# Two transfers of 2 MB for an expert's w_down in place of four of 1 MB, in a one-core MoE decoder layer

## What is computed

```python
def expert_chunk(args):
    toks, e = args
    hu = x_pad[toks] @ w_up[e] + b_up[e]
    return clamped_swiglu(hu) @ w_down[e] + b_down[e]
```

## Time and profile before

| what | value |
|---|---|
| runs | 1374.71, 1376.47 and 1380.66 us, median 1376.47 us |
| the profiled execution | 1378.88 us, its span 1377.0 us |
| mean granted TensorE clock | 0.937 of full speed |
| busy time | TensorE matmul 1179.8 us (86%), VectorE 311.5 us, ScalarE 257.5 us |
| read from HBM | 463.24 MB, 337 GB/s over the span |
| transfers of the MoE | w_up 256 of 1024 KB, w_down 128 of 1024 KB |

### The profile page before, as it was taken

The page is one execution under the profiler, slowest core; times in us unless marked ns, Lnnn a source line. Parts: engine busy times, 40 slices in busy tenths (PEclk is TensorE's granted clock), DMA queues, the critical chain, the costliest instruction groups (busy, mean ns, idle before and its releaser), DMA issues.

```text
span 1377.0 us, 21397 instructions
## 1 busy us (share of the span) xinstructions
PE 1179.8 (86%) x7951; PEld 586.2 (43%) x7952; DVE 311.5 (23%) x799; ACT 257.5 (19%) x389; POOL 0.2 (0%) x4
## 2 busy tenths in 40 slices
PE   5999899996979878988979998988988788788684
PEld 2845588854334325343334343343343333344232
DVE  1124543264111111212021111121211111111112
ACT  3034421213111211002111112021111211111111
POOL 0000000000000000000000000000000000000000
PEclk8899999998989977999989999999999989899898
DMA  9942384445669999647999999999999999999995
GB/s 335 381 162 91 120 323 176 176 157 211 245 229 419 419 416 416 245 175 309 416 375 382 417 418 418 419 416 417 410 420 418 418 418 417 417 417 418 418 419 234
DMA packets 102517, 465.00 MB, mean 338 GB/s; under 512 B 8172, under 2 KB 9540, under 8 KB 69574
## 3 DMA queue, kind: packets, MB, share of 16 engines
q1 hardware_dynamic: 100368, 461.52, 83.7%
q10 hardware_dynamic: 2102, 2.80, 0.6%
HBM read 463.24 MB, written 1.05 MB: 337 GB/s over the span
## 4 chain that ended last, share of the span: by engine, by line
PE 61%; DMA 22%; SPq 8%; issue 5%; DVE 4%; ACT 1%; DVEq 0%; ACTq 0%
PE psum L926 19%; PE psum L555 17%; DMA ring<-in_w_up 14%; PE psum L999 10%; DMA ring<-in_w_down 6%; PE psum L859 5%; SPq L513 4%; PE psum L918 3%; SPq L508 3%; PE psum L1017 2%; DMA ring<-in_ada_w 1%; PE psum L561 1%; PE psum L901 1%; DVE area L1658 1%; PE psum L962 1%
## 5 line engine op out<-in xcount | busy, mean ns | idle before, releaser
L926 PE MATMUL psum<-ring,area 128*32 128x512 f32 (+2 forms) x2432 | 395.6, 629 | 45.4 <-DMA ring<-in_w_up 45.4
L926 PEld LDWEIGHTS psum<-ring,area 128*32 128x32 f32 (+2 forms) x2432 | 105.3, 123 | 332.5 <-issue 255.7
L999 PE MATMUL psum<-ring,area 128*32 128x256 f32 (+2 forms) x2080 | 198.8, 422 | 25.7 <-DVE area L1643 14.8
L859 PEld LDWEIGHTS psum<-area 128*128 128x128 f32 x1056 | 128.1, 201 | 31.2 <-issue 31.2
L859 PE MATMUL psum<-area 128*128 128x128 f32 x1056 | 134.7, 288 | 0.3 <-DVE area L1549 0.3
L999 PEld LDWEIGHTS psum<-ring,area 128*32 128x32 f32 (+2 forms) x2080 | 71.8, 115 | 142.1 <-issue 79.6
L1618 DVE TENSOR_SCALAR area<-psum 128x256 f32<-128x256 f32 x51 | 21.7, 425 | 391.8 <-PE psum L926 391.8
L1207 ACT ACT_TABLE_LOAD x32 | 41.1, 1283 | 367.7 <-PE psum L901 367.7
L1219 ACT ACTIVATE area<-area 128x256 f32<-128x256 f32 x51 | 21.3, 417 | 405.5 <-DVE area L1618 405.5
L555 PE MATMUL psum<-hT,ring 128*128 128x256 f32 x370 | 81.9, 381 | 0.0
L555 PE MATMUL psum<-ring,hT 128*128 128x512 f32 (+1 forms) x192 | 77.8, 561 | 0.0
(11 more groups left out here) (196 smaller groups left out, 711.5 us busy)
## 6 DMA issues: line engine op xcount, KB each, us to landing
ring<-in_w_up SPq DMA_DIRECT2D x256, 1024.0 KB, 19.0
ring<-in_w_down SPq DMA_DIRECT2D x128, 1024.0 KB, 21.9
ring<-in_ada_w SPq DMA_DIRECT2D x12, 2048.0 KB, 16.4
ring<-in_w_in SPq DMA_DIRECT2D x11, 2048.0 KB, 19.6
ring<-in_w_out SPq DMA_DIRECT2D x2, 2048.0 KB, 10.3
ring<-in_w_branch_b SPq DMA_DIRECT2D x1, 2048.0 KB, 9.5
cst<-in_cst ACTq DMA_DIRECT2D x1, 1184.5 KB, 8.0
x_res<-in_x SPq DMA_DIRECT2D x1, 1024.0 KB, 5.2
```

Source lines behind the costliest of these rows:

```text
L859: ins = pe.matmul(ps[banks[i]][:, kk % 4 * P:(kk % 4 + 1) * P], h2[:, tt, kk * P:(kk + 1) * P], S[:, tt, 0:P], start=(tt == 0 and kk % 4 = ...
L926: ins = pe.matmul(ps[b][g * P // G:(g + 1) * P // G, 0:w], XT[:, kk, t0:t0 + P // G], wt[:, c0:c0 + w], start=False, stop=kk == KT - 1, sk ...
L999: ins = pe.matmul(ps[b][g * M:(g + 1) * M, 0:w], hidT[:, p, q * P + of * M:q * P + (of + 1) * M], down_weights(kk)[:, g * W + d * CW:g * W ...
```

## The change

Each expert's w_down comes in two transfers of 2 MB, one to a slot. Each brings four slices `kk`. SP issues the first when TensorE is through slices 0 to 3 of this expert's down stage, the second after the whole stage; TensorE waits for a landing before slice 0 and before slice 4. The bytes, their places in the slots, the rows of 4 KB in which they are read, and every arithmetic instruction stay as they were.

```diff
-        dn_tile = [sem(f"dn_tile{i}") for i in range(FT // 2)]
+        dn_tile = [sem(f"dn_tile{i}") for i in range(FT // 4)]
...
             def down_load(e, j):
-                to = slot(NF + 4 + j // 2)[:, j % 2 * 2 * D:(j % 2 + 1) * 2 * D].rearrange("p (k n) -> p k n", k=2)
-                src = a["w_down"][0][ds(e, 1), j * 2 * P:(j + 1) * 2 * P, :]
+                to = slot(NF + 4 + j)[:, :].rearrange("p (k n) -> p k n", k=4)
+                src = a["w_down"][0][ds(e, 1), j * 4 * P:(j + 1) * 4 * P, :]
                 sp.dma_start(to, src.rearrange("e (k p) n -> p (e k) n", p=P)).then_inc(dn_tile[j], 16)
...
-            for j in range(FT // 2):
-                if j % 2 == 0:
-                    sp.wait_ge(*released[names[NF + 4 + j // 2 - RING]])
+            for j in range(FT // 4):
+                sp.wait_ge(*released[names[NF + 4 + j - RING]])
                 down_load(0, j)
...
-                for j in range(FT // 2):
-                    if j < FT // 2 - 1:
-                        sp.wait_ge(dn_used, (FT // 2 - 1) * e - (FT // 2 - 1) + j + 1)
+                for j in range(FT // 4):
+                    if j < FT // 4 - 1:
+                        sp.wait_ge(dn_used, (FT // 4 - 1) * e - (FT // 4 - 1) + j + 1)
                     else:
                         sp.wait_ge(dn_full, MAX_D * e)
                     down_load(number, j)
...
                 for kk in range(FT):
-                    if kk % 2 == 0:
-                        pe.wait_ge(dn_tile[kk // 2], 16 * e + 16)
+                    if kk % 4 == 0:
+                        pe.wait_ge(dn_tile[kk // 4], 16 * e + 16)
...
-                    if kk % 2 and kk < FT - 1:
+                    if kk % 4 == 3 and kk < FT - 1:
                         ins.then_inc(dn_used, 1)
```

## The result

The change made the kernel slower by half a percent: 1383.47 us in the median of 20 runs (1377.09 to 1393.62) against 1376.23 us of before (20 runs, 1372.83 to 1384.23). The ratio is 1.0050, 95% interval 1.0034 to 1.0067. That is +7 us where I had forecast +2.6 us to 1379.1 us; the time lies within the range of 1374.0 to 1385.0 us. The profiled execution took 1387.22 us, its span 1385.4 us, 8.4 us above the one of before.

A forecast was written before the change was run, and what follows sets the result against it. TensorE was taken to bound one part, transfers another (416 GB/s from 728 us to 1361 us). Three terms of 0.86 us made +2.6 us on the 1376.47 us median: 1379.1 us, range 1374.0 to 1385.0 us.

The forecast's parts named there:

- The later half waits whole: Down stages at places 5, 8 and 31: 32 matmuls in 1.93 us behind the last landing, not 16; +0.86 us each.
- the first rival: After place 5, 527 to 546 us, the clock falls otherwise: 1372.3 us to 1384.4 us; 7% for loss, 6% for gain.
- The first half is released later, hidden by 11 us: Behind place 6, the worst: second 2 MB land 0.9 us later, by 616.1 us, but are needed after 627.05 us; cost nothing.
- The rule that before 728 us only delays from place 5 on count: Before 728 us a TensorE delay counts only after the last full transfer stretch (404 to 524 us), so from place 5.
- The cover at place 20: First w_up transfer there has 1.3 us to spare; place 17's 0.86 us lateness takes two thirds; costed at nothing.
- the second rival: The stream runs dry at place 20 (or 17 or 14), losing 1 to 3 us: 1380 to 1382 us; 6%.
- Fewer transfers, and the stream's rate: Last stream, 42 transfers fewer at 416 GB/s: gain of 0 to 2.5 us, taken as 0.
- the gain by a fixed time for each transfer: Rival in the last stream: each transfer holds the engines a fixed time, so 42 fewer give 2.5 us: 1376.6 us; 5%.
- the loss of 16 us: Rival in the stream: 2 MB transfers run slower, at 387 GB/s, 0.38 us x 42, 1395 us; 4%.
- The bound of 0.06 us: Upper bound on the stream's gain for 2 MB, from mixer landings 5.1 us apart against 5.04 us at 416 GB/s.
- The sum of 2.6 us: 0.86 us each at places 5, 8 and 31, all other parts at nothing; 65% for this sum.

The follow-up runs named there:

- holding the transfers: On the kernel before with only release by halves: the two 1 MB transfers after the down stage wait for the next expert's first transposes; 1383.14 us, ratio 1.0039.
- both edits at 1 MB: Kernel before with TensorE's wait for both landings of a half and release by halves, still four 1 MB transfers; 1381.67 us (1.0036), again 1382.75 us (1.0033).

## Why the prediction was right in sign and short in size

*The later half waits whole:* right in mechanism and place, mis-sized. The trace has the 32 matmuls behind the landing at places 5, 8 and 31. I took 1.93 us for them. At place 8 they took that; at place 5 3.29 us and at place 31 3.11 us. So the terms were 2.2, 0.8 and 2.0 us in place of three times 0.86. The reason is the clock, the subject of the first rival. But I had priced that only for the stretch from 527 to 546 us, where the granted clock hardly moved (0.61 for 0.64), and judged it unlikely since "the pattern in busy and idle time hardly differs". It differs: the longest waits of before in class 0 down stages are 1.48 us, and behind each of them 16 matmuls take 1.07 us; the new ones reach 3.27 us. Longer waits are not always followed by a low clock (the repeated run of the changed kernel has 1.93 us behind a wait of 2.73 us); that this is part of why the changed kernel's runs scatter over 16 us is likely and not shown. The first line is place 17 of before, the second place 22 of that repeated run:

```profile
939.54 1.07 PE L999 MATMUL psum<-ring,area 128*32 128x256 f32 x16 [1.46 <-DMA ring<-in_w_down]
...
1100.24 1.93 PE L998 MATMUL psum<-ring,area 128*32 128x256 f32 x32 [2.73 <-DMA ring<-in_w_down]
```

*The first half is released later, hidden by 11 us:* right for the transfers, wrong in what it left out. They land later (9.4 us after the issue and not the 7.2 us that I worked out) and still before they are needed. But the pause of TensorE in which they run is on the path, and it grew by 1.7 us (10.93 for 9.20). The releases by halves alone do that (10.65), and holding the transfers undoes it (9.31). I had put the later release at nothing because the weights are not needed for another 11 us, and had read this idle time as TensorE's affair, which transfers could not touch. The rule that before 728 us only delays from place 5 on count was too narrow as well: the stretch from 404 us on begins when the pause behind place 0 ends, so its 0.6 us count.

*The cover at place 20:* costed at nothing with 1.3 us to spare. Place 17 was late by 1.8 us more behind its landing and not by 0.86 (2.86 for 1.07), and by 0.9 us more in the sum that follows (2.09 for 1.15), again by the clock, and the stream ran dry: the second rival came with the first.

*Fewer transfers, and the stream's rate:* right. 416 to 417 GB/s inside the stream; neither the gain by a fixed time for each transfer nor the loss of 16 us appeared. (The bound of 0.06 us was worked out from landings that are shown to 0.1 us, so it was finer than its rows.) The fixed part of 2.0 us that the Trainium skill gives (*DMA: Bandwidth & Descriptors*, the section on the anatomy of one DMA) is its fit for transfers issued by GpSimd, and these are issued by SyncE. Something of that kind is seen only where the engines are idle: 4.7 us for 1 MB, whose bytes take 2.5 us at 416 GB/s. What size costs outside the stream (none to some 4 us) stays open.

The sum of 2.6 us was therefore a lower end: 2.5 us more from the clock at places 5 and 31, 1.7 us from the pause behind place 6, 1.5 us in the stream, most of it the break at place 20. The clock's parts differ from run to run. That the time fell inside the range is in part luck: its upper end was worked out from a clock that would fall in another stretch, and the pauses were not in it at all.

## What to carry to other kernels

Where a stream of loads sets the pace, what counts first about a transfer's size is how much work stands behind the landing of the last one: make the last piece small. For the early pieces a larger or smaller size made no difference here that shows. Cost the work behind a late landing at the clock that it may have after the wait, not only at the clock that it has now, and give every place at which a stream is nearly dry the same care. And a pause in which an engine waits for nothing that the profile shows can be on the path like any other wait, and can depend on the transfers that run in it: don't cost it as fixed.

## What the runs showed of the hardware

TensorE's pause after an expert of a rare class can depend on the w_down transfers that run in it. The idle time before the first transposes of the next expert, in us, over all fourteen profiles:

| w_down issued at the start of the pause | behind place 0 | behind place 6 |
|---|---|---|
| one transfer of 2 MB (3 profiles) | 7.31 to 7.90 | 10.93 to 11.39 |
| two of 1 MB (3) | 7.12 to 7.22 | 10.65 to 11.00 |
| one of 1 MB (3) | 6.83 to 7.21 | 9.20 to 10.00 |
| two of 0.5 MB (1) | 5.71 | 9.43 |
| one of 0.5 MB (1) | 6.69 | 8.92 |
| none, held (3) | 4.40 to 4.61 | 9.25 to 9.69 |

Behind place 0 any transfer lengthens it; behind place 6 only the second MB does. Behind place 9, the third such place, it is 6.81 to 7.21 us in all fourteen, whatever is held. That this pause is the fetch of TensorE's instructions is argued from where it stands, not shown, and why the three places differ is open.

A pause of the same kind came and went behind place 12. In the repeated profile of the changed kernel it reads

```profile
819.31 0.68 PE L900 MATMUL psum<-cst,area 128*128 128x128 f32 x2 [7.22 <-issue]
```

and in one of the two profiles with both edits at 1 MB it was there too, 7 us each; in all others the step from place 12 to 13 took 6.1 to 6.2 us and not 13. What decides it is open. The two profiles that have it are long ones (1389.94 and 1388.84 us, with medians of 1385.88 and 1382.75), so it may be behind some of the scatter between executions of one kernel.
